# Gate logits, first attention scores and output splits in new places: a two-block transformer step on one core

## What is computed

```python
def gla_inputs(gq, gk, gv, g_lr, gate_w, gate_b):
    ...
    r = g_lr.reshape(bsz, n, 2, GATE_RANK)
    logits = jnp.einsum('bnzr,zrk->bnzk', r, gate_w) + gate_b
    g = (jax.nn.log_sigmoid(logits.astype(jnp.float32)) / GATE_TAU).reshape(bsz, n, 2, B_HEADS, B_DK)
...
def diff_attention(q, k, v, lam):
    ...
        s = jnp.where(kpos[None, :] <= qpos[:, None], s, -jnp.inf)
        p = jax.nn.softmax(s, axis=-1)
        a = p[:, :, 0] - lam * p[:, :, 1]
        return jnp.einsum('bhqk,bhkd->bhqd', a.astype(v.dtype), v)
...
def second_block(x, ...):
    for layer in range(DEPTH):
        if layer % 2 == 0:
            x = x + even_mixer_2(rms_norm_2(x, even_norm[i]), even_w_in[i], even_w_out[i])
        else:
            x = x + diff_mixer(rms_norm_2(x, odd_norm[i]), ..., lambda_init)
        x = x + conv_ffn(rms_norm_2(x, ffn_norm[layer]), ...)
```

## Time and profile before

| | |
|---|---|
| runs | 2397.42, 2394.99, 2391.75 us; median 2394.99 |
| profiled execution | 2395.21 us, its span 2393.4 us |
| TensorE busy | 2309.7 us, 97% |
| VectorE, ScalarE, GpSimd busy | 48%, 41%, 16% |
| mean granted clock of TensorE | 0.988 |
| chain that ended last | TensorE 90%, ScalarE 5%, VectorE 4%, issue 1% |

### The profile page before, as it was taken

The page is one execution under the profiler, slowest core; times in us unless marked ns, Lnnn a source line. Parts: engine busy times, 40 slices in busy tenths (PEclk is TensorE's granted clock), DMA queues, the critical chain, the costliest instruction groups (busy, mean ns, idle before and its releaser), DMA issues.

```text
span 2393.4 us, 32492 instructions
## 1 busy us (share of the span) xinstructions
PE 2309.7 (97%) x12406; PEld 1780.0 (74%) x12406; DVE 1147.9 (48%) x1778; ACT 978.8 (41%) x1634; POOL 374.8 (16%) x252
## 2 busy tenths in 40 slices
PE   7999999898999999999999999999999989999998
PEld 4888765366868877777766788888877667888886
DVE  5000453744452103753447466674544564766645
ACT  5111426545244424643236443332342663433422
POOL 2233000200323331030000300004300003000143
PEclk9999999999999999999999999999999999999999
DMA  8122330110132222122210233323322103323331
GB/s 319 53 62 62 105 134 9 42 52 1 45 115 71 62 74 81 55 86 88 79 62 2 81 95 97 95 89 97 97 88 79 45 8 90 94 91 96 97 97 45
DMA packets 51437, 187.95 MB, mean 79 GB/s; under 512 B 5707, under 2 KB 6091, under 8 KB 51052
## 3 DMA queue, kind: packets, MB, share of 16 engines
q1 hardware_dynamic: 51308, 186.16, 23.9%
HBM read 184.04 MB, written 2.10 MB: 78 GB/s over the span
## 4 chain that ended last, share of the span: by engine, by line
PE 90%; ACT 5%; DVE 4%; issue 1%; DMA 0%; POOL 0%; SPq 0%; DVEq 0%; ACTq 0%; POOLq 0%
PE PS L656 7%; PE PS L654 7%; PE PS L655 6%; PE PS L1832 4%; PE PS L2505 3%; PE PS L2506 3%; PE PS L2507 3%; PE PS L1859 3%; PE PS L1524 3%; PE PS L1845 3%; PE PS L608 3%; PE PS L609 3%; PE PS L607 3%; PE PS L814 2%; PE PS L816 2%; PE PS L815 2%
## 5 line engine op out<-in xcount | busy, mean ns | idle before, releaser
L654 PE MATMUL PS<-H_HI,W_SPLIT 128*128 128x512 f32 x672 | 265.5, 395 | 0.0
L656 PE MATMUL PS<-H_HI,W_SPLIT 128*128 128x512 f32 x672 | 264.9, 394 | 0.0
L655 PE MATMUL PS<-H_LO,W_SPLIT 128*128 128x512 f32 x672 | 264.5, 394 | 0.0
L503 POOL TENSOR_TENSOR W_SPLIT<-WT,W_SPLIT 128x1024 fp32r<-128x1024 f32 x43 | 104.6, 2433 | 612.8 <-ACT W_SPLIT L492 495.5
L469 ACT ACTIVATE W_SPLIT<-WT 128x1024 fp32r<-128x1024 f32 x80 | 84.8, 1060 | 267.3 <-PE PS L656 267.3
L1027 POOL TENSOR_TENSOR OUT_HALF<-WT,OUT_HALF 128x512 fp32r<-128x512 f32 x48 | 71.2, 1486 | 652.6 <-ACT OUT_HALF L985 652.6
L2860 DVE TENSOR_TENSOR W_SPLIT<-WT,W_SPLIT 128x1024 fp32r<-128x1024 f32 x80 | 98.0, 1225 | 150.1 <-ACT W_SPLIT L469 150.0
L2846 DVE TENSOR_TENSOR G_LO<-SB,G_HI 128x512 fp32r<-128x512 f32 x43 | 100.4, 2335 | 109.0 <-ACT G_HI L2666 109.0
L655 PEld LDWEIGHTS PS<-H_LO,W_SPLIT 128*128 128x128 f32 x672 | 126.0, 188 | 30.3 <-issue 0.5
L654 PEld LDWEIGHTS PS<-H_HI,W_SPLIT 128*128 128x128 f32 x672 | 126.2, 188 | 29.9 <-issue 0.5
L656 PEld LDWEIGHTS PS<-H_HI,W_SPLIT 128*128 128x128 f32 x672 | 126.2, 188 | 29.8
(11 more groups left out here) (355 smaller groups left out, 5358.9 us busy)
## 6 DMA issues: line engine op xcount, KB each, us to landing
WT<-weights SPq DMA_DIRECT2D x313, 512.0 KB, 3.5
SB<-weights SPq DMA_DIRECT2D x13, 512.0 KB, 12.6
XT<-tokens SPq DMA_DIRECT2D x4, 768.0 KB, 7.1
SB<-rpb SPq DMA_DIRECT2D x8, 384.0 KB, 3.7
HT<-rpb SPq DMA_DIRECT2D x8, 384.0 KB, 4.4
out<-HT SPq DMA_DIRECT2D x4, 512.0 KB, 3.1
SB<-late SPq DMA_DIRECT2D x1, 1280.0 KB, 6.0
SB<-con SPq DMA_DIRECT2D x1, 1248.0 KB
```

Source lines behind the costliest of these rows:

```text
L503: g.tensor_tensor(w[:, 1, :], W[:, (g0 + t) % SLOTS, :], w[:, 0, :].bitcast(F32), ALU.subtract).then_inc(sem("w_lo"), 1)
L654: pe.matmul(PS[:, s, :], hi, H_HI[:, c, :], start=(c == 0), stop=False)
L655: pe.matmul(PS[:, s, :], hi, H_LO[:, c, :], start=False, stop=False)
L656: last = pe.matmul(PS[:, s, :], lo, H_HI[:, c, :], start=False, stop=(c == KC - 1))
```

## The change

1. The logits of direction 0 stand between the halves of the first projection's last tile. They and the later sums move from banks 4 to 6 to banks 5 to 7, and what used bank 7 uses bank 4. ScalarE's copy of the last tile comes behind the softplus of direction 0, and sums and transposes are in a new order.
2. `Window.split_hi` and `split_lo` take three of the five chunks of unit 3 behind unit 1.
3. `Projected.pe` does the scores of the first two steps (`ahead=2`) before value tile 23, for both attentions of the second model, and ScalarE their exponentials before the copies of the values' second half. The masked scores (`sm_at`) move to another place in SBUF, since the old one still holds the inputs.
4. In `Differences.pe`, two chunks of the output stand ahead of the last unit's sums, and five behind them.
5. Lambda is made in front of the even projection, and the function table is loaded before both down projections instead of before the second and before the differential attention.

```diff
+        def project_halves_pe(pe, name, n, ntok, first=None, midway=None):
             a0, d0, split = ev_base[name]
             w0 = half_at[name]
             if a0:
@@ -608,6 +609,8 @@
                             pe.matmul(dst, hi, HN_LO[:, c, at:end], start=False, stop=False)
                             last = pe.matmul(dst, lo, HN_HI[:, c, at:end], start=False, stop=(c == KC - 1))
                     last.then_inc(sem("tile_used" if h else "half_used"), 1)
+                    if midway and h == 0 and isinstance(q, int) and 8 * q + s == n - 1:
+                        midway()
             tiles(name, n, body)(pe)
...
 
-            def pe(self, pe):
+            def pe(self, pe, att):
                 pe.wait_ge(sem("evac_act"), after(self.prev)[0])
                 first_two_pe(pe, self.name, self.d0 - 8)
                 for t in range(2, 24):
@@ -801,6 +804,11 @@
                         last.then_inc(sem("col_summed"), 1)
                     if t == 5:
                         pe.wait_ge(sem("rc_log"), self.k + 1)
+                    if t == 23:
+                        self.heads(pe)
+                        self.first_values(pe)
+                        for s in range(att.ahead):
+                            att.scores(pe, s)
                     pe.wait_ge(sem("w_low"), self.low0 + t + 1)
                     hi, lo = (W_SPLIT[:, t % 2, k, :] for k in range(2))
...
                         half = (k - 16) // 4
+                        if half:
+                            self.heads(act)
+                            for s in range(att.ahead):
+                                att.exps(act, s)
                         act.wait_ge(sem("rc_ready"), self.k + 1)
                         for tb in range(4):
```

```diff
-            def ahead_pe(self, pe):
-
-                for c in range(KC - 1):
+            def ahead_pe(self, pe, chunks=range(KC - 1)):
+
+                for c in chunks:
                     self.chunk_pe(pe, 0, c)
...
 
-                for k in {3: range(0, 5), 5: range(5, 7), 7: range(7, 8)}.get(u, ()):
+                for k in {1: range(0, 3), 3: range(3, 5), 5: range(5, 7), 7: range(7, 8)}.get(u, ()):
                     if k >= 4:
                         act.wait_ge(sem("at_out"), att_mla.b["out"] + 2 * (k - 4) + 2)
+                    elif k == 3:
+                        act.wait_ge(sem("at_out"), att_mla.b["out"] + 4)
                     elif k == 0:
-                        act.wait_ge(sem("at_out"), att_mla.b["out"] + 4)
+                        act.wait_ge(sem("at_out"), att_mla.b["out"] + 2)
...
@@ -2087,9 +2101,10 @@
                     if 0 <= s - self.lag - 1 < self.S:
                         self.values(pe, s - self.lag - 1)
                     if s - self.lag - 2 == self.final[-1]:
-                        self.following.ahead_pe(pe)
+                        self.following.ahead_pe(pe, range(0, 2))
                     if s - self.lag - 2 in self.final:
                         self.sums(pe, self.final.index(s - self.lag - 2))
+                self.following.ahead_pe(pe, range(2, KC - 1))
 
```

```diff
                       lambda i, a, c: VTE[:, c, 128 * i + 64 * a:128 * i + 64 * a + 64], 0.125, PE_AT, 2, lambda i: OFE[:, i, :],
-                      mask=causal_mask(lambda u: u // 4), values_in=qkv_e2.values, sm_at=PE_AT + 5120, rt_at=PE_AT + 6144, dve_takes=(0,))
+                      mask=causal_mask(lambda u: u // 4), values_in=qkv_e2.values, sm_at=BIG + 27136, rt_at=PE_AT + 6144, dve_takes=(0,), ahead=2)
         assert att_e.end <= PE_AT + 5120
         LAMS = SB[:, BIG + 24064:BIG + 24064 + 256]
         NLAM = STAT[:, 24:25]
         att_df = Differences([(i, CAUSAL) for i in range(8)], causal_q, causal_k,
                              lambda i, a, c: VTE[:, c, 128 * i:128 * i + 128], 0.125, PE_AT, 3, lambda i: OFE[:, i, :],
-                             mask=causal_mask(lambda u: 0), values_in=qkv_df.values, sm_at=PE_AT + 5120, rt_at=PE_AT + 6144, sq_at=PE_AT + 6656, wide=512)
+                             mask=causal_mask(lambda u: 0), values_in=qkv_df.values, sm_at=BIG + 27136, rt_at=PE_AT + 6144, sq_at=PE_AT + 6656, wide=512, ahead=2)
 
 
...
-                    last = pe.matmul(PS[:, (4, 1)[z] + b // 2, (b % 2) * 256:(b % 2) * 256 + 256], GR[0:33, b * 128:b * 128 + 128],
+                    last = pe.matmul(PS[:, (5, 1)[z] + b // 2, (b % 2) * 256:(b % 2) * 256 + 256], GR[0:33, b * 128:b * 128 + 128],
                                      GWB[:, 256 * z:256 * z + 256], start=True, stop=True)
                 last.then_inc(sem("logits"), 1)
 
...
-            pe.wait_ge(sem("evac_act"), after("ev_in")[0] - 1)
-            pe.wait_ge(sem("evac_dve"), after("ev_in")[1])
-            logits(0)
-            turn(0)
-            wait_projected(pe, "ev_in")
-            for u in range(1, 4):
-                turn(u)
-            logits(1)
-            for u in range(4, 9):
-                turn(u)
-            pe.wait_ge(sem("gla_turned"), 9)
-            for z in range(2):
-                pe.wait_ge(sem("gates"), z + 1)
-                if z:
-                    pe.wait_ge(sem("exp_b"), 1)
+            def first_logits():
+                pe.wait_ge(sem("con_in"), 32)
+                pe.wait_ge(sem("gate_one"), 1)
+                pe.wait_ge(sem("evac_act"), after("ev_in")[0] - 1)
+                pe.wait_ge(sem("evac_dve"), after("ev_in")[1])
+                logits(0)
+
+            def inclusive(z):
                 for b in range(6):
                     for c in range(2):
                         at = 768 * c + 128 * b
-                        last = pe.matmul(PS[:, 4 + at // 512, at % 512:at % 512 + 128], GLOG[z][:, b, 128 * c:128 * c + 128],
+                        last = pe.matmul(PS[:, 5 + at // 512, at % 512:at % 512 + 128], GLOG[z][:, b, 128 * c:128 * c + 128],
                                          con_("tri", 128, 128 * z), start=True, stop=True)
                 last.then_inc(sem("gate_b"), 1)
-                if z:
-                    pe.wait_ge(sem("exp_d"), 1)
-                else:
-                    pe.wait_ge(sem("gates"), 2)
+
+            def strict(z):
                 for b in range(6):
                     last = pe.matmul(PS[:, 1 + b // 2, (b % 2) * 256:(b % 2) * 256 + 256], con_("strict", 128, 128 * z),
                                      GLOG[z][:, b, :], start=True, stop=True)
                 last.then_inc(sem("gate_d"), 1)
+
+            project_halves_pe(pe, "ev_in", EV_CHUNKS, N, midway=first_logits)
+            turn(0)
+            wait_projected(pe, "ev_in")
+            logits(1)
+            pe.wait_ge(sem("gates"), 1)
+            inclusive(0)
+            for u in range(1, 5):
+                turn(u)
+            pe.wait_ge(sem("gates"), 2)
+            strict(0)
+            for u in range(5, 9):
+                turn(u)
```

```diff
                     act.activation(PROJ[:, q * 8 + s, :], result(s, N), ACT.Copy).then_inc(sem("evac_act"), 1)
-            split_halves_act(act, "ev_in", EV_CHUNKS, take_ev)
+            split_halves_act(act, "ev_in", EV_CHUNKS, take_ev, last=False)
 
 
             for z in range(2):
                 act.wait_ge(sem("logits"), z + 1)
                 G6 = GLOG[z].rearrange("p b n -> p (b n)")
-                bank = (4, 1)[z]
+                bank = (5, 1)[z]
                 chain.link(act.activation(G6, PS[:, bank:bank + 3, :].rearrange("p b n -> p (b n)"), ACT.Abs))
                 chain.link(act.activation(G6, G6, ACT.Exp, scale=-1.0))
                 act.activation(G6, G6, ACT.Ln, bias=1.0).then_inc(sem("softplus"), 1)
-            SB_ = PS[:, 4:7, :].rearrange("p b n -> p (b n)")
+                if z == 0:
+                    take_ev((EV_CHUNKS - 1) // 8, (EV_CHUNKS - 1) % 8)
+            SB_ = PS[:, 5:8, :].rearrange("p b n -> p (b n)")
             SD = PS[:, 1:4, :].rearrange("p b n -> p (b n)")
             for z in range(2):
...
                         act.activation(down_g(l, t)[0], G[:, t, :], ACT.Copy).then_inc(sem("g_hi"), 1)
-                if l == 1:
-                    act.preload_act_table_set("natural_log_exp_and_others")
+                act.preload_act_table_set("natural_log_exp_and_others")
                 tiles(f"down{l}", FC, down)(act)
 
-            qkv_e2.act(act, out_e2)
+            act.wait_ge(sem("lam_dots"), 1)
+            act.activation(STAT[:, 28:30], STAT[:, 26:28], ACT.Exp).then_inc(sem("lam_exp"), 1)
+            qkv_e2.act(act, out_e2, att_e)
             att_e.act(act)
             out_e2.act(act)
             ffn_act(0)
-            qkv_df.act(act, out_df)
-            act.wait_ge(sem("lam_dots"), 1)
-            act.activation(STAT[:, 28:30], STAT[:, 26:28], ACT.Exp).then_inc(sem("lam_exp"), 1)
-            qkv_df.heads(act)
-            act.preload_act_table_set("natural_log_exp_and_others")
+            qkv_df.act(act, out_df, att_df)
...
+            gates(0)
             for u in range(9):
                 v.wait_ge(sem("gla_turn"), u + 1)
```

(9 more changed lines are left out.)

67 lines of the change are left out of this document (32 added, 35 removed).

## The result

The changed kernel took 2370.86 us (median of 6 runs, 2365.86 to 2379.56) beside 2394.52 us before (6 runs): a ratio of 0.9914, 95% interval 0.9891 to 0.9937. The forecast was 2378.0 with a range of 2374 to 2386.5. The profiled execution took 2365.86 us, a span of 2364.0.

The account below looks back on a forecast made before the run. TensorE, busy 97% of the span, was taken as the bound, so only its pauses and the low clock behind them count; 2.0 + 2.9 + 3.5 + 4.0 + 4.9 = 17.3 us off 2395.2 gave 2378 us, range 2374 to 2386.5.

Parts of the forecast that it names:

- 1 gates: Gate logits between the last tile's halves: ScalarE and VectorE start earlier, worth 2.0 us, bounds 0 and 3.5.
- 2 splits: First block's output splits: 2.37 us wait removed, 0.7 added elsewhere, slow stretch gone; 2.9 us, bounds 1.2 and 3.0.
- 3 even attention: First scores before the even attention's last value tile: waits and low clock go, 3.5 us, bounds 1.7 and 3.8.
- 4 start of differential: First scores before the differential attention's last value tile: earlier scores, no slow stretch; 4.0 us, bounds 1.5 and 4.4.
- 5 its end: Differential attention's end, five chunks behind the sums: pause minus 3.55, slow stretch minus 1.35; 4.9 us, bounds 3.2 and 5.3.
- the lambda sums and the table loads: Moved lambda sums and table preload counted at nothing, hidden by idle time; without these covers 1.3 us cost.
- (b): Rival: ScalarE sets the attentions' pace, so both starts give 0 instead of 7.5 us; 2385.5 us, chance 0.12.
- (c): Rival: slower, TensorE waits before value tile 23 for rotated heads and first value copy; about 2401 us, chance 0.02.
- (a): Rival: pauses go but the clock stays low behind short matmuls, 6.1 us kept; 2384 us, chance 0.17.
- The slow stretch: Low clock behind 564.43 us, at the first block's output splits, should go with the wait: 1.65 us.
- The walk: Step-by-step full-clock timing from first logits to second inclusive sums, which start 2.8 us earlier than in the profile.
- the old second logits lost about 1 us there: Low-clock loss in the old gate order, cited when taking 2.0 us instead of the 2.8 us of steps.

Follow-up runs that it names:

- fill2_b: Kernel before with unused matmuls (1, 5, 10, 7, 7 and 15), sized to end inside the waits, put into six TensorE waits; median 2384.4 us, ratio 0.9974.
- p_chunks: Kernel before with only five chunks of the last output projection moved behind the sums of the differential attention; median 2385.0 us, ratio 0.9972.
- fill_b: Kernel before with unused matmuls put into six TensorE waits, so many that they outlasted the waits; median 2397.4 us, ratio 1.0020.
- m_chunks: Changed kernel with all seven output chunks again ahead of the sums of the differential attention; median 2372.1 us, ratio 0.9931.
- fill2_end: Kernel before with 15 unused matmuls in the 3.59 us wait behind the last sums of the differential attention; median 2395.0 us, ratio 1.0006.
- p_splits: Kernel before with only the output splits of the first block spread over more units; median 2392.0 us, ratio 0.9988.
- fill3_a: Changed kernel with five TensorE waits filled with unused matmuls; 2369.47 us, ratio 0.9900.

## Why the prediction was right and wrong

Stage lengths repeat to 0.1 us between traces once the stretches are counted, so each part can be priced from traces that differ in it alone. Steps means at the full clock, stretch the slow part behind the pause.

| part | forecast | measured | from |
|---|---|---|---|
| 1 gates | 2.0 | 0.9 steps; stretches 0.7 to 4.2 more | logits' place to scan: 28.8 us (one of nine traces without the part), 29.5 to 33.0 in the others; 27.9 in eight of ten with it, 29.5 in two |
| 2 splits | 1.3 + 1.65 | 2.5 steps + 0.6 | first attention 132.3 us (fill2_b) and 129.8 (changed), both at 1.00; step by step, before against changed, 3.1 at this place |
| 3 even attention | 3.5 | 1.9 steps + 1.6 | stage 278.2 us with a stretch (two of nine traces without the part), 276.6 without; 274.7 with the part, every time |
| 4 start of differential | 4.0 | 2.9 steps + 0.9 | stage 278.4 us (p_chunks) less 272.9 is 5.5, of which 1.7 is a stretch at 1950; from the first scores to the second unit's last step p_chunks takes 22.2 us and fill_b, without a stretch there, 21.2 |
| 5 its end | 4.9 | 3.6 steps + 1.1 | stage 277.5 us (m_chunks) and 272.9 (changed) give 4.6; 283.1 (before) and 278.4 (p_chunks) 4.7; 283.1 and 282.0 (fill2_end) the stretch |

**Right.** From this table's traces and the earlier trace rows, parts 2 to 5 came out at 3.1, 3.5, 3.8 and 4.7 us against 2.9, 3.5, 4.0 and 4.9, taken between the trace before and the changed kernel's first. What was to show each step is there: waits gone, new waits smaller than forecast, nothing for the lambda sums and the table loads (the stage between the attentions took 367.1 us before and 367.0 after). Rival (b) fell with the stage of 272.9 us, (c) with no wait in front of either value tile, and (a) in the main: each part is in ten traces, and in these no stretch stays behind the removed pauses of parts 2 to 5, and two stay around the logits. What (a) rested on is not refuted, though: the clock did fall behind small waits and small matmuls, as shown above.

**Right in part by luck.** Part 3's 3.5 us needs the stretch behind the old pause, and only two of nine traces have one; on the average of traces it is worth 2.3. In part 2 two errors cancel. The slow stretch was put at 1.65 us, but taking it away at full clock brings out another wait of TensorE, 0.96 us for the exponentials (fill2_b, 558 us), which the slow matmuls had covered; so the stretch cost 0.6, and the steps, which were put at 1.3, were worth 2.5, since the change removes that wait too. The reason given for the stretch to go was also a misreading: "single waits of about 1 us in this phase are followed by none", but in that same trace the stretches at 476 and 510 us stand behind waits of 1.32 and 1.04 us.

**Wrong in its makeup: part 1.** The walk gave 2.8 us by setting full-clock steps against a trace that held a long slow stretch there, and "the old second logits lost about 1 us there" took off too little. At the full clock the old order takes 28.8 us and the new 27.9: the reordering is worth 0.9 us, all else is the clock. In this pair of traces the two came to 31.1 - 27.9 = 3.2 us.

**The step that failed** is the base of the sum: "The sum is made against the profiled execution, 2395.2 us ... The median of the runs shown is 2395.0, so nothing needs to be shifted". The five places in the pair of traces add up to 3.2 + 3.1 + 3.5 + 3.8 + 4.7 = 18.3 us, against 17.3 forecast; 11.8 of them are steps and 6.5 stretches, where the sum had 11.2 and 6.1. (The product fell by 7.8 us only, since it takes off half of every stretch, also where the stretch cost less.) The spans of the profiled executions are 29.4 us apart. The other 11.1 us lie where nothing was changed: the scan 2.0, the latent stage 3.9, the first attention's other stretches 3.1, a stretch at 1950 1.7, the start 1.2, all else 0.1, less 0.9 around 669 us, where the changed kernel's trace has a stretch and the one before has none. I had the trace's low clock only behind the pauses at stake, 6.1 us, and held the other 22 of its 28.5 us to be a constant of the kernel. It is not: the kernel before loses 14 to 34 us, run by run. Its three runs that I took for the base lay 2.3 us above its median of 109, and the first six of the changed kernel 2.9 us under its median of 18. The sounder statement of the result is 2392.7 to 2373.8, 18.9 us; the three measured ratios, 0.9914, 0.9918 and 0.9915, come to 19.6 to 20.6 us. My sum from the sounder base would have been 2375.4.

That accounts for the 6.4 us between 17.3 and 23.7: 1.6 us a gain that is larger than my sum (18.9), and 4.8 us where the first runs of each kernel fell. The range failed because it held bounds for each place and none for the runs; its lower end would have needed some 3 us more.

**What stays open.** The low clock of the changed kernel is 11.5 us smaller on the mean than before. The five places hold some 7 to 8 us of that by the traces (part 1 about 2, part 2 up to 1.7, part 3 in two of nine traces, parts 4 and 5 3.4). The same gap shows in time: averaged over the traces with and without each part, the five places are worth 2.4 + 3.0 + 2.3 + 3.7 + 4.7 = 16.1 us, the change as a whole 19.2 plus or minus 2.5. Whether the other 3 to 4 us come from the change, because one stretch makes the next likelier, or are the spread of 18 runs, these runs can't tell. Nor did I find what decides, at one and the same wait, for or against a stretch.

## What to carry to other kernels

Before pricing an edit by one trace, list where that trace holds low-clock stretches, and compare the product of span and clock over several runs: a place is worth its pause plus its stretch times how often it is there, and the stretches elsewhere belong into the range, not into the base. Behind a stretch, look for the next wait: if slow matmuls cover it, taking the stretch away brings it out. Compare stages by their lengths in traces that differ in one part; here that resolved 0.1 us where medians of twelve runs resolved 3. A wait that can't be removed can be filled: matmuls that nobody uses, written where the next accumulation starts anew and sized to end inside the wait, were worth 4 to 5 us over four waits. Look into the trace whether the filling landed in its wait; one of these did not.

## What the runs showed of the hardware

- A stretch at 1.2 GHz cost 1.6 us at the even attention (stage 278.2 or 276.6 us), 2.9 behind the thirteenth head (latent stage 125.5 or 122.6 us), and only 0.6, 0.9 and 1.1 at the places of parts 2, 4 and 5. It is neither certain nor rare: the wait of 2.42 us at 442 us had none behind it in the changed kernel's first trace, and one in its second and third.
- TensorE need not stand still for the clock to fall: it was busy for 3.00 of 3.00 us ahead of the stretch at 301 us in p_splits, and for 6.00 of 6.00 ahead of the one at 246 us in fill3_a.
- Work that nobody uses, put into a wait, keeps the clock up behind it: at 41 to 44 us 14 of 14 traces without it have a stretch, none of five with it.
- One program, unchanged, ran from 2382.1 to 2400.1 us in 109 runs with clocks of 0.994 to 0.986; the changed one had runs at 2367.3 (clock 0.997) and 2379.0 (0.992) side by side on one chip.
- A 128-column matmul of two operands that hold ordinary 32-bit numbers (ones by the identity) took 0.22 us a piece in a row of 24, and a value matmul of the differential attention 0.26 us (four in 1.06 us). Each stands in the trace as two entries (x48, x8), a transpose of 128 columns as one.
